# Even layer's entry: norm weights and biases on turned columns, first projection on unscaled tokens, six pieces loaded in the experts

## The reference, cut to what matters

```python
# end of the first block
x = layer_norm(ALPHA * x + moe + ple, ln2_w, ln2_b)
# even layer
hn = x * rsqrt(mean(x * x) + EPS) * norm_even_g
q, k, v, u, z_a, z_b = split(hn @ w_in_even)      # each 1024 wide
o_a = attention(q, k, v) * silu(z_a)
y   = gelu(s5_ssm(u))                             # a complex linear recurrence over time
o_b = y * sigmoid(y @ w_glu + b_glu) * silu(z_b)
x   = x + concat(o_a, o_b) @ w_out_even
# odd layer follows, and a last norm
```

## Time and profile before

| | us |
|---|---|
| median of 3 runs (3214.1 to 3218.9) | 3215.3 |
| the profiled execution, first to last instruction (span) | 3213.3 |
| PE busy | 3035.3 (94%) |
| DVE busy | 1550.1 (48%) |
| ACT busy | 837.7 (26%) |
| POOL busy | 266.6 (8%) |

### The profile page before, as it was taken

The page is one execution under the profiler, slowest core; times in us unless marked ns, Lnnn a source line. Parts: engine busy times, 40 slices in busy tenths (PEclk is TensorE's granted clock), DMA queues, the critical chain, the costliest instruction groups (busy, mean ns, idle before and its releaser), DMA issues.

```text
span 3213.3 us, 42675 instructions
## 1 busy us (share of the span) xinstructions
PE 3035.3 (94%) x18308; PEld 2171.3 (68%) x18308; DVE 1550.1 (48%) x1862; ACT 837.7 (26%) x926; POOL 266.6 (8%) x245
## 2 busy tenths in 40 slices
PE   8999999899999999999999999799999999999998
PEld 6787777899987733333333333288768878997886
DVE  4465544674555513222222322438886554444655
ACT  3342222544433311011101100110001334443443
POOL 2042111000000000000000000054330000000000
PEclk9999988999998999999999999899999999999899
DMA  7543221456564599999999999743333465887443
GB/s 243 152 136 99 74 67 55 119 161 180 177 228 152 211 413 425 425 425 425 425 425 425 425 425 425 291 140 118 117 119 118 144 175 122 184 189 158 99 158 138
DMA packets 215216, 722.10 MB, mean 225 GB/s; under 512 B 16170, under 2 KB 18634, under 8 KB 164716
## 3 DMA queue, kind: packets, MB, share of 16 engines
q1 hardware_dynamic: 210716, 702.22, 62.6%
q0 software_dynamic: 3216, 14.97, 1.3%
q10 hardware_dynamic: 1088, 2.10, 0.2%
HBM read 717.13 MB, written 2.10 MB: 224 GB/s over the span
## 4 chain that ended last, share of the span: by engine, by line
PE 73%; DMA 12%; DVE 10%; ACT 4%; issue 1%; POOL 0%; DVEq 0%; ACTq 0%
PE psum L137 72%; DMA t<-in_w_up 11%; DVE t L283 7%; ACT t L254 2%; PE psum L143 1%; DVE t L294 1%; ACT t L256 1%; DVE t L298 0%; DVE t L306 0%; ACT L254 0%; POOL t L328 0%; DVE t L269 0%; ACT L256 0%; DMA t<-in_x 0%; DVE t L275 0%
## 5 line engine op out<-in xcount | busy, mean ns | idle before, releaser
L137 PE MATMUL psum<-t,t 128*128 128x256 f32 (+10 forms) x17230 | 2941.4, 380 | 125.5 <-DVE t L283 69.3
L137 PEld LDWEIGHTS psum<-t,t 128*128 128x128 f32 (+4 forms) x17230 | 2080.0, 175 | 948.1 <-issue 580.3
L283 DVE TENSOR_TENSOR t<-t,t 128x1024 fp32r<-128x1024 f32 (+6 forms) x642 | 785.0, 1223 | 502.1 <-ACT t L254 469.1
L254 ACT ACTIVATE t<-t 128x1024 fp32r<-128x1024 f32 (+8 forms) x521 | 528.5, 1014 | 924.5 <-PE psum L137 661.2
L283 DVE TENSOR_TENSOR t<-t,psum 128x1024 f32<-128x1024 f32 (+3 forms) x265 | 246.4, 930 | 739.5 <-PE psum L137 439.0
L254 ACT ACTIVATE t<-psum 128x1024 f32<-128x1024 f32 (+5 forms) x278 | 213.5, 768 | 1408.7 <-PE psum L137 1310.4
L328 POOL TENSOR_TENSOR t<-t,t 128x1024 f32<-128x1024 f32 (+9 forms) x125 | 209.0, 1672 | 545.4 <-DVE t L283 258.2
L283 DVE TENSOR_TENSOR t<-psum,t 128x1024 f32<-128x1024 f32 (+5 forms) x125 | 100.2, 802 | 131.6 <-PE psum L137 103.0
L143 PE MATMUL psum<-t,t 128*128 128x128 f32 (+1 forms) x566 | 87.7, 294 | 32.1 <-DVE t L294 18.4
L143 PEld LDWEIGHTS psum<-t,t 128*128 128x128 f32 (+1 forms) x566 | 67.3, 149 | 69.6 <-issue 39.8
L83 POOL DMA_DIRECT2D t<-in_s_lr x1 | 0.6, 574 | 1185.1 <-DVE t L306 1185.1
(11 more groups left out here) (65 smaller groups left out, 237.9 us busy)
## 6 DMA issues: line engine op xcount, KB each, us to landing
t<-in_w_gate SPq DMA_DIRECT2D x128, 1024.0 KB, 16.9
t<-in_w_up SPq DMA_DIRECT2D x128, 1024.0 KB, 18.4
t<-in_w_down SPq DMA_DIRECT2D x128, 1024.0 KB, 17.4
t<-in_w_in SPq DMA_DIRECT2D x160, 512.0 KB, 4.3
t<-in_w_in_odd SPq DMA_DIRECT2D x128, 512.0 KB, 5.3
t<-in_w_in_even SPq DMA_DIRECT2D x96, 512.0 KB, 3.8
t<-in_w_out SPq DMA_DIRECT2D x32, 512.0 KB, 4.7
t<-in_w_pg SPq DMA_DIRECT2D x32, 512.0 KB, 4.1
```

Source lines behind the costliest of these rows:

```text
L137: ins = self.e.matmul(o, l, r, start=start, stop=stop, skip_group_check=True)
L254: self.put(self.e.activation(o, i, f, scale=scale), event)
L283: self.put(self.e.tensor_tensor(o, a, b, op), event)
```

## The change

- `second_norm` takes only mean and inverse deviation of `x` (one operation for each 128 by 512 part, `centred`). Weight and bias are applied to the turned columns, where they are one number for each partition: DVE's `gained` writes `hTe` with weight times gain and bias times gain from PSUM, ACT squares with weight as scale and bias as bias. The two engines take the halves of a group in opposite order, each waiting for the other.
- POOL adds the squares (three operations of 128 by 1024, one of 512, one of 256 columns); PE then needs one product with the ones.
- PE starts `ev.u` on tokens that aren't scaled yet, with the turning of the later groups between the pieces. The scale is applied by DVE where `ev.u` leaves PSUM (`states_in`), and to `hTe` in place (`scaled_tokens`, four operations) once `ev.u` has read each part.
- `s5_setup` now stands before `token_scales`, `states_in` and `scaled_tokens`; `s5()`, with `pad(0)`, behind them.
- `x` itself still needs weight and bias for the residual: POOL loads both rows and makes eight operations of 128 by 1024 at the exit of the layer, behind the wait for `ev.oT 3`; DVE waits for `("l2.rest", ci)` ahead of each `add_and_sum`.
- SP loads the first six pieces behind the last expert weights, into room that the experts have left; the buffer `xg` moves for that. The two rows that SP loaded there go.

```diff
@@ buffers
+        l2c = at(invm_at + 800, 32)...     # ln2 weight and bias as columns
+        l2g = at(invm_at + 832, 32)...     # the same times gains[0]
+        xg = [alloc(4096)...]              # now ahead of yb, selT, selw, gu
-        loads += [("ln2_w", 0, 0), ("ln2_b", 0, 0)]
+        l2w, l2b = [at(s5_at + 2048 * k, 2048) for k in range(2)]
@@ PE, even
+                def turned_pairs(j):
+                    w = pe.take("ev.T", j, of=(0, 3)).rearrange("p (k b t) -> p k b t", b=2, k=4)
+                    pe.wait_ge(("l2.x", j), j > 1 and ("ev.hTs", j - 2) or None)
+                    ...
+                turned_pairs(0)
+                for j in range(4):
+                    if j < 3:
+                        turned_pairs(j + 1)
+                    for i in (2 * j, 2 * j + 1):
+                        pe.wait_ge(("ev.hT", 2 * i + 1))
+                        some(first, 1)
+                ps = pe.take("r1.sum", of=(0, 3))
+                pe.wait_ge(("r1.squares",), ("ev.hTs", 3))
+                pe.mm(ps[:, 0:256], ones[:, 0:128], squares[0][:, 0, :], True, True, event=("r1.sum",))
                 some(first, 8)
+                # ev.q: its first 8 pieces wait for ("ev.hTn", i // 2)
@@ DVE
+                def centred(j):
+                    for b in range(2):
+                        xc = x[:, b, 512 * j:512 * j + 512]
+                        v.ts(xc, xc, mv[:, b, 0:1], inv[:, b:b + 1], ALU.subtract, ALU.mult, ...)
+                def gained(j):
+                    v.wait_ge(("ev.T", j))
+                    for k in range(4):
+                        i = 4 * j + k
+                        if k == 2:
+                            v.wait_ge(("r1.square", j, 1))
+                        v.ts(hTe[:, i, :]..., ps[:, k], l2g[:, 0, i:i + 1], l2g[:, 1, i:i + 1],
+                             ALU.mult, ALU.add, event=("ev.hT", i))
+                centred(0)
+                centred(1)
+                v.wait_ge(("meet", "pe", 7), ("meet", "act", 7), ("meet", "pool", 7))
+                for j in range(4):
+                    gained(j)
+                    if j < 2:
+                        centred(j + 2)
+            def states_in(ci):
+                v.wait_ge(("ev.u", ci))
+                v.tt(uT[:, 4 * ci:4 * ci + 4, :], v.bank("ev.u", ci)..., over_tokens(4), ALU.mult, ...)
+            def scaled_tokens(g4):
+                v.wait_ge(("used", "s", stream.turn + 9 + 2 * g4))
+                h4 = hTe[:, 4 * g4:4 * g4 + 4, :]
+                v.tt(h4, h4, over_tokens(4), ALU.mult, event=("ev.hTn", g4))
             def even():
                 s5_setup()
+                token_scales()
+                states_in(0)
+                for g4 in range(4):
+                    scaled_tokens(g4)
+                states_in(1)
                 s5()
             for z in pads:
                 v.mset(z, 0.0)
-            scaled_tokens()
             even()
             for ci in range(4):
+                v.wait_ge(("l2.rest", ci))
                 add_and_sum("ev.out", ci)
@@ ACT, instead of one Square and one Copy of a whole group
+                for k in (2, 3, 0, 1):
+                    i = 4 * j + k
+                    if k == 0:
+                        a.wait_ge(("ev.hT", i + 1))
+                    a.activation(squares[j][:, k, :]..., ps[:, k], ACT.Square, bias=l2c[:, 1, i:i + 1],
+                                 scale=l2c[:, 0, i:i + 1], event=("r1.square", j, k // 2))
@@ POOL
+            for j in range(1, 4):
+                g.wait_ge(("r1.square", 0, 0), ("r1.square", j, 0))
+                g.tt(squares[0], squares[0], squares[j], ALU.add)
+            g.tt(squares[0][:, 0:2], squares[0][:, 0:2], squares[0][:, 2:4], ALU.add)
+            g.tt(squares[0][:, 0], squares[0][:, 0], squares[0][:, 1], ALU.add, event=("r1.squares",))
             ...
+            g.wait_ge(("ev.oT", 3), ("ev.oT", 5))
+            g.load(("landed.l2",), [(l2w, along("ln2_w")), (l2b, along("ln2_b"))])
+            g.wait_ge(("landed.l2",))
+            for ci in range(4):
+                cs = slice(512 * ci, 512 * ci + 512)
+                g.tt(x[:, :, cs], x[:, :, cs], two(l2w[:, cs], 512), ALU.mult)
+                g.tt(x[:, :, cs], x[:, :, cs], two(l2b[:, cs], 512), ALU.add, event=("l2.rest", ci))
             g.stage("odd")
@@ SP
+            s.wait_ge(("mo.gu", 27))
+            pieces(stream, stream.turn, stream.turn + 4)
+            s.wait_ge(("mo.gu", 31))
+            pieces(stream, stream.turn + 4, stream.turn + 6)
```

More of the change, by code:

```diff
@@ L166, in __init__ @@
         self.raw, self.hi, self.lo = bufs
+        self.raw = [self.raw[(k - turn) % len(self.raw)] for k in range(len(self.raw))]
         self.known = known
@@ L484, in build @@
         top[0] = 0
+        xg = [alloc(4096).rearrange("p (j s) -> p j s", j=16) for _ in range(2)]
         yb = [alloc(1024) for _ in range(2)]
@@ L496, in build @@
         place = {key: i for i, key in enumerate(loads)}
-        loads += [("ln2_w", 0, 0), ("ln2_b", 0, 0)]
-        l2w, l2b = [slots[(len(loads) - 2 + k) % 10] for k in range(2)]
         top[0] = free_from
@@ L1339, in tensor_program @@
             pe.stage("even")
-            total = pe.take("r1.sum", of=(0,))
-            for j in range(5):
-                if j < 4:
-                    turn_columns("ev.T", x, j, ("l2.x", j), of=(1, 2, 3))
-                if j:
-                    pe.wait_ge(("r1.square", j - 1))
-                    for k in range(4):
-                        pe.mm(total[:, 0:256], ones[:, 0:128], squares[(j - 1) % 2][:, 256 * k:256 * k + 256],
-                              j == 1 and k == 0, j == 4 and k == 3, event=("r1.sum", j - 1) if k == 3 else None)
             even()
@@ L1726, in second_norm @@
                 v.ts(spread, var, 1e-5, None, ALU.add, event=("l2.var",))
-                first = place["w_down", 31, 3] + 1
-                v.wait_ge(("l2.std",), ("landed.w", first), ("landed.w", first + 1))
+                v.wait_ge(("l2.std",))
                 v.rcp(inv, stdev)
-                for ci in range(4):
-                    cs = slice(512 * ci, 512 * ci + 512)
+                def centred(j):
                     for b in range(2):
-                        xc = x[:, b, cs]
-                        v.stt(xc, xc, mv[:, b, 0:1], l2w[:, cs], ALU.subtract, ALU.mult)
-                        v.stt(xc, xc, inv[:, b:b + 1], l2b[:, cs], ALU.mult, ALU.add, event=("l2.x", ci) if b else None)
@@ L1910, in scattered @@
                                     sums(v, 24 * b, 2 * c + h, b, 1024 * h + 512 * c)
+                v.wait_ge(("landed.gains",))
+                for k in range(2):
+                    v.tt(l2g[:, k, :], l2c[:, k, :], gains[0], ALU.mult)
                 for ex in range(34):
```

68 lines of the change are left out of this document (39 added, 29 removed).

## The result

The changed kernel takes 3237.4 us (median of 4 runs, 3235.7 to 3242.5). The kernel before took 3217.1 us (4 runs, 3214.1 to 3222.6). The ratio is 1.0066, 95% interval 1.0049 to 1.0083: slower by about 20 us. The profiled span is 3235.1 us, against 3213.3.

A forecast was written before the change was run, and what follows sets the result against it. PE was taken as the bound, with 73% of the chain that ended last. Entry 0, exit stall 12, clock and splits 4.5 gave +16.5 us: span 3213.3 to 3229.8, plus 2.0 around it, 3232 us; 8-in-10 range 3217 to 3243.

The forecast's parts named there:

- PE's start: Entry: PE's first `ev.u` record at 2085.4, 16.7 us earlier, with a cold clock costing 1.5 us.
- Head start at the end of `ev.u`: Entry: PE finishes `ev.u` at 2144.8 instead of 2160.28, 15.5 us ahead.
- POOL's chain starts at 2119.8 to 2121.8: Entry, behind `s5_setup`: against 2121.31 before, 1.5 us earlier at best; POOL may hold DVE's memsets up to 2 us.
- `turn_b(1)` doesn't move: Entry: POOL's phases hold DVE's first rotation, so `turn_b(1)` stays at 2175.7; gain 0 us, ends -3 and +4.
- PE's second stall: Entry, ahead of `turn_b(1)`: PE idle 10 to 13 us, using up part of its head start.
- Behind `turn_b(1)` PE's work is the same: After the entry: PE's work behind `turn_b(1)` is unchanged, with no term in the sum.
- Split 2.2: Exit: DVE's split of piece 6, queued behind the wait, runs 2583.7 to 2585.9 beside POOL; bounds 1.23 and 3.3.
- Clock and slow splits 4.5 us: Exit, behind PE's stall: cold clock and splits slowed beside POOL's other six operations cost 4.5 us, ends 1 and 9.
- The first (POOL doesn't limit): Entry: DVE's order sets the gain, `turn_b(1)` 11 us earlier at 2164.7; net +5.5, 3221 us; chance 0.12.
- The second: Entry: the head start at `turn_b(1)` outlasts the exit's stall; net -6.1, 3209 us; chance 0.08.
- The third: Exit: dearer, rows land as late as 13.9 us and POOL and DVE take strict turns; +28, 3243 us; chance 0.08.
- The fourth: Exit: the wait costs nothing because `l2.rest 0` comes before 2574.1; 3215 us; chance 0.03.

The follow-up runs named there:

- e4: Changed kernel with the four `scaled_tokens` products cut from 128 by 1024 to 128 by 32, most of `hTe` left without token scale; 3233.8 us, one run.
- e2: Changed kernel without the exit's row loads, POOL's eight operations and DVE's wait, so weight and bias are left out of the residual; 3222.8 us, ratio 1.0014.
- e7: Changed kernel with SP loading the first six pieces only behind the end of the experts; 3233.6 us, ratio 1.0045 to the kernel before.
- e9: Changed kernel with the residual's weight and bias applied by POOL beside the attention, behind the recurrence's last gelu, one row at a time; 3220.9 us, ratio 1.0004.
- e3: Changed kernel with `pad(0)` straight behind `s5_setup`, ahead of `token_scales`, `states_in` and `scaled_tokens`; 3239.1 us, ratio 1.0054 to the kernel before.
- before_again: The kernel before, unchanged, run once more against itself; 3219.0 us, ratio 1.0004.
- e11: The kernel before with only the change's edits upstream of the last expert stage (buffer placing, constants' loads, two small products); 3218.6 us, ratio 0.9994.
- e5: Changed kernel with `s5_setup` ahead of `gained(3)`, and PE instead of POOL summing the fourth group's squares; 3234.3 us, ratio 1.0048 to the kernel before.
- e6: Changed kernel with the residual's weight and bias applied by POOL straight behind `make_phases(7)`, one row at a time; 3227.2 us, ratio 1.0024 to the kernel before.
- e8: Changed kernel with five later pieces instead of two ahead of `turn_b(1)`, and one less in each of slices 1 to 3; 3227.6 us, ratio 1.0024.

## Why the prediction was right, point by point

The forecast was 3232 us, with 3217 to 3243 as its range. The median is 3237.4. The direction, the size and the two places were right. "On the old scale" means with the 4.09 us of late arrival taken off. In the order of its steps:

- **PE's start.** `ev.u` forecast at 2085.4, with the first four `centred` at 0.55 us each. They took 2.29 / 4 = 0.57. The first record started at 2089.09, or 2085.0 on the old scale. The clock came back sooner than the forecast had it: granted 0.50 in 2085 to 2089 and 0.90 in 2089 to 2093, and the first 32 records took 7.46 us, 0.5 over the 6.94 of full clock instead of 1.5.
- **Head start at the end of `ev.u`.** Forecast 15.5 us, measured 17.4: 2105.04 + 42.04 = 2147.1, that is 73.6 us behind the last expert product against 91.0.
- **POOL's chain starts at 2119.8 to 2121.8.** It started at 2123.43, or 2119.3 on the old scale, just under the lower end. The memsets weren't held. Each took 0.59 with gaps of 0.20, though POOL was busy from 2107.74 on. Here the Trainium skill's rule on DVE instructions with at most one SBUF input and outside the two-port modes (SBUF — State Buffer, "Who interferes with whom") agrees with the trace. The two small products behind the memsets were held instead (0.61 and 0.51 us where they took 0.19), so 0.7 us of my bound of 2 came true.
- **POOL held by DVE's products.** Forecast 2 us out of 0 to 5. e4 measured 3.5 us, 0.9 for each of four products.
- **`turn_b(1)` doesn't move.** Forecast 0, with -3 and +4; measured -0.3. The chain started 2.0 us earlier than in the kernel before and took 47.3 us to DVE's first rotation, where its phases were ready after 43.5. That is 1.8 us later, and in the kernel before DVE had not needed them for another 1.65 us, because it waited for PE. So the rotation comes 0.2 us later, and the copies behind it take 3.59 us instead of 4.04. That three terms of 2 to 4 us come to nothing is partly luck; that POOL now holds the rotation is not. PE's second stall was forecast at 10 to 13 us and was 13.07. The first was forecast at 6 to 9 us, with 6 as a sign to look for; it was 3.71 + 1.32, so this sign failed. It failed in the adding up: the prediction's own terms (1.25, 1.25, 1 to 4.04 and the copy's 1.3) give 4.8 to 7.8.
- **Behind `turn_b(1)` PE's work is the same.** The clock was left out of this step. From `turn_b(1)` to POOL's load behind `ev.oT 3` is 395.3 us, where it was 394.2: +1.15 us (+0.9 by PE's own rows, 386.4 against 385.5). PE starts that stretch at granted clock 0.50 behind its 13 us of standing, and its 160 records took 36.75 us instead of 35.90. But this is one profile. With the same stall e2, e7 and e9 took 385.1 to 385.2 us and 35.4 to 35.6 for the 160 records, no more than the kernel before. So the term is 0 to 1 us, and it varies from execution to execution.
- **Load 9.5 us** (7.4 to 13.9): 2574.84 to 2582.54 is 7.7. **Two POOL operations 4.3**: 4.8. **Split 2.2**: it took 1.23 us, because it started 0.04 us ahead of POOL's next operation. So the stall, forecast at 12, was 9.62 us.
- **Clock and slow splits 4.5 us** (1 to 9). From `ev.oT 3` to the odd layer it is 15.72 us longer. With 9.62 off, 6.1 are left: 2.72 are the second gap, 1.9 are the 48 records before it (13.07 us, where four pieces take 11.2), and 1.8 are the 264 behind it (63.40 us, where 22 pieces take 61.6); by PE's own rows the exit is 15.96 us longer, so these three add up to it within 0.1. The clock has its part (granted 0.56 in 2588.6 to 2592 and 0.65 in 2604 to 2608), the splits the other. The exclusive lock of the Trainium skill (SBUF — State Buffer, "Who interferes with whom"), in which the later one fully blocks, agrees with the trace. Of the first six splits one came ahead of POOL's operation and took 1.23 us. The five that started within one of POOL's took 3.18, 3.21, 3.22, 2.87 and 3.18, against the 3.6 that the prediction had worked out from that rule. PE needs a piece every 2.8 us, so it runs out. By that rule this term was to be 5 to 7 us, and 6.1 is what it was: the 4.5 that I took, with splits of 2.25 to 3.3, was too low.
- **Sum.** Forecast +16.5, measured -0.27 + 1.15 + 15.72 = +16.6. That it fits so closely is partly luck: the stall was taken 2.4 us too long, the terms behind it 1.6 us too short, 1.15 us was missing, and e3 and e7, which change nothing at the exit, have +15.0 and +14.6. The further 5.4 us between 3232 and the median lie outside of the layer. 1.8 of them are the kernel before, whose median is 3217.1 now and was 3215.3. Seen in the profiles, 4.1 us stand before the layer and 1.1 behind it; three profiles without the entry's edits (before, before_again, e11) spread over 3.3 us at that place, and e11 shows that the upstream edits cost nothing. The rest isn't settled: e2's local time is that of the kernel before (582.8), and it was timed 0.14% (0.02 to 0.25%) slower, while e9, with the same local time, was at 1.0004.

The rivals. The first (POOL doesn't limit) is refuted by DVE's 17.17 us wait for POOL and by e3. The second fails at the same place: it needed `s5.setup` 10 us earlier and DVE's scaling out of the way of `pad(0)`. e5 shows that with 9 us earlier, and the scaling still in front, only 4.1 arrive; both together weren't tried. The third was too dear in both of its parts. The fourth needed `l2.rest 0` within about 4 us of `ev.oT 3` (2574.1 less 2569.85 is 4.25 us, not the 4.05 of the prediction, and 3.0 with the split's 1.23 taken off); it took 12.5.

## What to carry to other kernels

An engine that starts earlier gains only what the slowest chain behind it lets through, so give its idle time work that is otherwise done later. Here the 17 us of head start were worth 0 until three pieces were moved into the gap of 13 us, and then 11.4 us. On an engine that runs in order, a wait costs what is queued behind it: put the feeding of the bound engine ahead of it, or let the awaited work be done where its engine has slack and so has the one that it slows (here DVE beside POOL).

## What the runs showed of the hardware

- DVE's scans are held by POOL's big products as its two-input products are. In e6 a scan of 128 by 256 that began within one of them took 2.66 us, 0.69 alone; a product of 128 by 1024 took 3.26 to 3.39, 1.23 alone. It goes the other way too: POOL's products took 2.6 to 2.8 us beside the scans and 3.2 beside the products, where the first of them took 2.3, and four DVE products lengthened POOL's chain by 3.5 us (e4).
- One of the eight `centred`, with one tensor and two scalar columns as its inputs, was held as well: it began at 2093.82, 0.07 us ahead of POOL's adding of squares, and took 2.69 us where the others took 0.55. PE didn't wait for it. The first split at the exit began 0.04 us ahead of POOL's operation and wasn't held, so the starts in the profile don't tell by themselves which of two goes first.
- A row load of 1024 KB from POOL's queue took 5.0 us from issue to POOL's first use (`ln2_w` in e9, 2455.21 to 2460.19) and 7.7 us (`ln2_b`, 2471.35 to 2479.03), each alone in its queue. In e6 it was 6.5 and 6.6 us, and in the changed kernel both rows, issued together, took 7.7. Why they differ wasn't tried.
- Filling the gap ahead of `turn_b(1)` brought back the clock as well: granted 1.00 in the 4 us behind it (e8), against 0.57 in the kernel before, where the gap was about as short (2.35 us) but came behind 48 records and not 96. The slice behind it took 35.44 us instead of 37.11.
